# Shift-scale row on TensorE, sums moved between attention heads, a tenth pair of weight buffers

## The chip, the cores and the metric

The kernel runs on one core of a Trainium2 chip. Its time is the device time of one execution in microseconds (us), here 1450.13 us as the median of three executions (1447.05 to 1450.35). A core has TensorE (PE in the profile, matrix products, with PEld for its weight loads), VectorE (DVE, elementwise work and sums), ScalarE (ACT, activations and copies), GpSimd (POOL) and SyncE (SP). The engines run side by side and wait for each other by semaphores. Weights come from HBM by DMAs that SP and POOL issue; sixteen DMA engines carry them. Matrix results lie in eight banks of PSUM, everything else in SBUF.

## The reference

One layer of a diffusion transformer in float32, for 256 latent tokens and 256 context tokens of width 2048.

```
mod = silu(c) @ w_mod + b_mod                 # 6 parts of 2048: shift, scale, gate, shift, scale, gate
n_l = rmsnorm(x) * (1 + mod[1]) + mod[0]
z_l = n_l @ w_in                              # q, k, v, gMLP u and v, conv a and g
z_c = n_c @ w_in[:, k and v]                  # context tokens
out = concat(window_attention(q, k, v, k_c, v_c, sink),
             chunk_gmlp(u, v), conformer_conv(a, g)) @ w_out
h   = x + mod[2] * out
m   = rmsnorm(h) * (1 + mod[4]) + mod[3]
y   = grouped_moe(m)                          # router picks 2 of 16 experts per token
h   = h + mod[5] * y                          # expert e: silu(m @ w_gate) * (m @ w_up) @ w_down
```

Each expert has 24 MB of weights (w_gate, w_up and w_down, 8 MB each), and every expert that has tokens is read. The kernel moves 559.56 MB in all.

## The kernel before

**Order of the work.** `make_schedule` writes TensorE's order by hand. First come the modulation rows for shift and scale of the mixer, with the input projections for `a`, `g` and the first half of q (`Q0_`) between them. Then come the projections `KV_`, `Q1_`, `V_`, `U_` (16 steps of 128 rows each, four to a 1 MB chunk of weights), with the attention heads 0 to 7 spread over `Q1_` to `U_`, then `w_out` in 4 groups of 4 chunks (L753), the router (L772 to L821), the first expert job (always expert 15), and a loop over jobs. A job is one expert with a block of up to 96 of its tokens: 8 chunks of w_gate and 8 of w_up (L932 for up to 32 rows, L937 for 64), then 8 of w_down (L956, L962). The loop takes jobs in pairs, a small one that leads and a larger one.

**Buffers and who fills them.** SP issues all weights, in program order, so an issue that waits holds up those behind it. `ring` has 8 slots of 1 MB. Up to `w_out` the chunks of `CHUNK_STEPS` go round 6 of them; the other two (slots 6 and 7) hold four half-slots of 512 KB, which POOL fills with `w_half` for VectorE. For the expert jobs the memory is cut into pairs of 2 MB, `job_pairs`: 0 is ring slots 6 and 7, pairs 1, 2, 3 are slots 0 to 5, and pairs 4 to 8 lie over buffers that fall free in the course of the layer (`once` is pair 8). The first job uses nine of them (`first_pairs`), the loop six (`next_pairs`).

**The rest of the modulation.** The last four parts of the modulation go two ways. Part 5 (the gate of the experts) is made on TensorE, in 16 steps ("gate", L596) of four products each in four column groups. Parts 2, 3 and 4 are six halves of 1024 columns, and each half is a sum over 16 blocks of 128 rows: VectorE adds one block at a time, `sum_rows(n)` (L1311), 96 sums in all, and TensorE then sums over the partitions with a product with ones ("half", L583 for halves 0 and 1, L587 for 2 to 5). `sum_rows(n)` stands at fixed places in VectorE's program: 11 of the 96 ahead of head 1, 7 in the heads, 25 behind them, and 17, 16, 13 and 7 in the four groups of `w_out`.

**Who starts a half.** The two accumulators `halves` are used in turn. Before the first block of half i, POOL runs `start_half(i)` (L490, L492): it waits until half i-2 has been summed over the partitions by TensorE (`half_free`), clears the buffer and loads the bias, and only then issues that block (L498). POOL issues block m once VectorE has added block m-4. TensorE does half 0 right behind the scores of head 4 (`halves = {4: 0, 7: 1}`).

**Attention per head.** TensorE makes the scores (L687, L688), VectorE the maximum (`head_max`, L1445), ScalarE the exponentials, VectorE adds one block and then scales (`head_probs`, L1454), TensorE transposes the probabilities (L699) and multiplies by v (L706). Three steps of a projection (12 rows of the trace, L640) stand between scores and transposes.

## Time and profile before

| | |
|---|---|
| median of three executions | 1450.13 us (1447.05 to 1450.35) |
| the profiled execution | 1449.17 us, of which 1447.4 us are the span of the trace |
| PE busy | 1299.3 us (90%) |
| DVE busy | 423.1 us (29%) |
| ACT / POOL busy | 209.1 us / 73.6 us |
| DMA | 559.56 MB, mean 387 GB/s |
| mean granted TensorE clock | 0.975 of full speed |

How to read it: times in the trace count from the start of the span. The page cuts the span into 40 equal slices of 36.2 us; a digit is a busy share in tenths. A timeline row has start, duration, engine, line, operation, operands, count of merged instructions and, in brackets, how long the engine had been idle before it and what ended that. Ends of matmuls are modelled, so neighbouring rows overlap by up to 0.2 us; where it matters, starts are subtracted from starts. A row of the stretches has, for each engine, busy time and number of instructions, then the granted clock, the DMA share and GB/s. A row of the chain of waits in order of time has start, duration and what was on the chain.

### The profile page before, as it was taken

To read this page: it belongs to the slowest core of one execution; us is meant where nothing else is said; L and a number is where in the kernel's file an instruction comes from. 1 tells how busy PE (TensorE), PEld (TensorE's weight loads), DVE (VectorE), ACT (ScalarE), POOL (GpSimd) and SP (SyncE) were. 2 spreads that over 40 slices of the span, in tenths; PEclk is the share of its full clock that TensorE was granted. 3 is DMA by queue.
4 is the path that set the end of the run, shared out by engine and by line. 5 is a ranking of instruction groups with operands and counts; after the bars stand their busy time and mean duration, and the time that the engine had idled before them with its cause. 6 is when DMAs were issued, how large, how long until landed. Compare 5 with 4: busy or idle time off the path is not lost.

```text
span 1447.4 us, 20580 instructions
## 1 busy us (share of the span) xinstructions
PE 1299.3 (90%) x8742; PEld 618.0 (43%) x8743; DVE 423.1 (29%) x803; ACT 209.1 (14%) x488; POOL 73.6 (5%) x138
## 2 busy tenths in 40 slices
PE   6899999999989998999999999997887887878857
PEld 4556444545445465433632543442442442333223
DVE  2002885877666340202111201021110111111112
ACT  2002101343001133100200110110110110011001
POOL 0001301121322000000000000000000000000000
PEclk9999999999999899999999999999999999999988
DMA  9999659687998899999999999999999999999996
GB/s 380 409 420 384 252 233 397 217 279 271 346 377 313 334 368 426 427 426 424 427 427 415 418 428 427 411 428 427 429 427 428 427 430 428 429 429 428 427 428 263
DMA packets 57450, 559.56 MB, mean 387 GB/s; under 512 B 6688, under 2 KB 6816, under 8 KB 20768
## 3 DMA queue, kind: packets, MB, share of 16 engines
q1 hardware_dynamic: 42768, 504.35, 83.4%
q0 software_dynamic: 14320, 52.01, 9.9%
q10 hardware_dynamic: 288, 2.10, 0.3%
q8 instruction: 60, 0.98, 0.3%
q14 instruction: 14, 0.11, 0.0%
HBM read 556.34 MB, written 2.10 MB: 386 GB/s over the span
## 4 chain that ended last, share of the span: by engine, by line
PE 52%; DMA 39%; DVE 5%; issue 2%; ACT 1%; DVEq 0%; SPq 0%; ACTq 0%
DMA ring<-w_up_dram 11%; PE ps L932 9%; DMA ring<-w_gate_dram 9%; PE ps L937 8%; PE ps L640 7%; DMA ring<-w_half_dram 6%; PE ps L899 5%; PE ps L956 4%; DMA ring<-w_down_dram 4%; DMA big<-w_up_dram 4%; PE ps L962 3%; DVE once L1311 3%; DMA ring<-w_in_dram 3%; PE ps L634 2%; PE ps L645 2%
## 5 line engine op out<-in xcount | busy, mean ns | idle before, releaser
L1680 DVE TENSOR_TENSOR big<-ps,big 128x1024 f32<-128x1024 f32 x60 | 70.7, 1220 | 306.5 <-PE ps L885 161.0
L937 PE MATMUL ps<-ring,big 128*64 128x512 f32 x560 | 132.9, 608 | 22.1 <-DMA ring<-w_up_dram 10.6
L640 PE MATMUL ps<-ring,big 128*128 128x512 f32 x320 | 148.1, 602 | 2.9 <-DMA ring<-w_in_dram 2.3
L1311 DVE SCALAR_TENSOR_TENSOR once<-ring,silu_c,once 128x1024 f32<-128x1024 f32 x96 | 123.2, 1283 | 62.9 <-DMA ring<-w_half_dram 57.2
L899 PEld LDWEIGHTS ps<-probs,big 128*128 128x128 f32 x1024 | 119.2, 191 | 44.3 <-issue 37.6
L899 PE MATMUL ps<-probs,big 128*128 128x96 f32 x1024 | 129.8, 280 | 1.9 <-DVE probs L1684 1.9
L932 PE MATMUL ps<-ring,early 128*32 128x256 f32 x1408 | 90.4, 406 | 30.8 <-DMA ring<-w_up_dram 18.3
L753 PE MATMUL ps<-ring,big 128*128 128x512 f32 x240 | 109.5, 614 | 0.0
L640 PEld LDWEIGHTS ps<-ring,big 128*128 128x128 f32 x320 | 58.4, 191 | 70.4 <-issue 64.8
L937 PEld LDWEIGHTS ps<-ring,big 128*64 128x64 f32 x560 | 36.2, 137 | 104.6 <-issue 66.9
L962 PE MATMUL ps<-ring,once 128*64 128x512 f32 x336 | 77.5, 598 | 3.4 <-DMA ring<-w_down_dram 3.4
L932 PEld LDWEIGHTS ps<-ring,early 128*32 128x32 f32 x1408 | 44.3, 115 | 76.9 <-DMA ring<-w_up_dram 22.6
L956 PE MATMUL ps<-ring,once 128*32 128x512 f32 x576 | 73.2, 602 | 0.3 <-DMA ring<-w_down_dram 0.3
L753 PEld LDWEIGHTS ps<-ring,big 128*128 128x128 f32 x240 | 46.9, 198 | 56.9 <-issue 56.9
L1216 ACT ACTIVATE big<-ps,modcol,scale_ffn 128x96 f32<-128x96 f32 x112 | 39.1, 429 | 206.1 <-PE ps L899 206.1
L1712 DVE TENSOR_TENSOR once<-ps,early 128x512 f32<-128x512 f32 x12 | 8.3, 692 | 192.3 <-PE ps L956 125.4
L498 POOL DMA_DIRECT2D ring<-w_half_dram x96 | 51.1, 532 | 256.9 <-DVE once L1311 256.9
L1216 ACT ACTIVATE early<-ps,modcol,scale_ffn 128x96 f32<-128x96 f32 x144 | 50.3, 429 | 77.7 <-PE ps L899 77.7
L634 PE MATMUL ps<-big,ring 128*128 128x256 f32 x256 | 58.5, 382 | 1.6 <-DMA ring<-w_in_dram 1.6
L937 PE MATMUL ps<-big 128*64 128x512 f32 x224 | 52.4, 600 | 7.5 <-DMA big<-w_up_dram 5.0
L634 PEld LDWEIGHTS ps<-big,ring 128*128 128x128 f32 x256 | 47.8, 190 | 12.5 <-DMA ring<-w_in_dram 4.7
L932 PE MATMUL ps<-big,early 128*32 128x256 f32 x608 | 40.4, 414 | 13.9 <-DMA big<-w_up_dram 7.9
(320 smaller groups left out, 1094.0 us busy)
## 6 DMA issues: line engine op xcount, KB each, us to landing
ring<-w_down_dram SPq DMA_DIRECT2D x48, 2048.0 KB, 23.4
ring<-w_up_dram SPq DMA_DIRECT2D x46, 2048.0 KB, 23.0
ring<-w_gate_dram SPq DMA_DIRECT2D x33, 2048.0 KB, 22.1
ring<-w_half_dram POOLq DMA_DIRECT2D x96, 512.0 KB, 5.9
big<-w_up_dram SPq DMA_DIRECT2D x18, 2048.0 KB, 22.3
ring<-w_mix_dram SPq DMA_DIRECT2D x32, 1024.0 KB, 11.0
late<-w_down_dram SPq DMA_DIRECT2D x16, 2048.0 KB, 23.7
big<-w_gate_dram SPq DMA_DIRECT2D x15, 2048.0 KB, 25.4
```

The source lines that it names most:

```text
L498: pool.dma_start(half_slots[:, m % HALF_SLOTS, :], w_half[m]).then_inc(half_in[m % HALF_SLOTS], 16)
L634: mm = pe.matmul(Z[b + q // 2][:, (q % 2) * SEQ:(q % 2 + 1) * SEQ], w[:, q * P:(q + 1) * P], nT[:, k, 0:SEQ], start=(k == 0 and q % 2 == 0 ...
L640: mm = pe.matmul(ps[:, b + t, :], nT[:, k, t * P:(t + 1) * P], w, start=(k == 0), stop=(k == KT - 1))
L753: mm = pe.matmul(ps[:, b + t, :], mixT[:, k, t * P:(t + 1) * P], w[:, i, :], start=(k == 0), stop=(k == KT - 1))
L899: mm = pe.matmul(Yb[:, i, at:at + BLK], tokens[:, t, k * P:(k + 1) * P], one_hot[:, t, :], start=(t == 0), stop=(t == TT - 1))
L932: mm = pe.matmul(out_b[0][BASE * f:BASE * (f + 1), :], rows[0][:, k, :], w[:, kk, f * 256:(f + 1) * 256], start=(k == 0), stop=(k == KT - 1))
L937: mm = pe.matmul(out_b[1][REST * f:REST * (f + 1), :], rows[1][:, k, :], w[:, kk, f * N:(f + 1) * N], start=(k == 0), stop=(k == KT - 1))
L956: mm = pe.matmul(Db[0][BASE * q:BASE * (q + 1), :], hT[0][:, (i % 2) * P + BASE * (i // 2):(i % 2) * P + BASE * (i // 2 + 1)], w[:, q * N: ...
L962: mm = pe.matmul(Db[1][REST * (q // 2):REST * (q // 2 + 1), q % 2, :], hT[1][:, (i % 4) * P + REST * (i // 4):(i % 4) * P + REST * (i // 4 ...
L1216: last = act.activation(to[:, k, :], Yb[:, k // 4, at:at + BLK], ACT.Identity, bias=modcol[:, 3, k, 0:1], scale=scale_ffn[:, k:k + 1])
L1311: stt(total, half_slots[:, m % HALF_SLOTS, :], silu_c[:, m % KT, 0:1], total, ALU.mult, ALU.add) \
L1680: tt(y, Yb[:, 2 * h:2 * h + 2, :].rearrange("p a n -> p (a n)"), y, ALU.add).then_inc(summed, 1)
```

## The change

1. Half 5 (the second half of part 4, the scale of the experts' norm) leaves VectorE (`DVE_HALVES = 5`, 80 sums instead of 96). TensorE makes it in 8 steps ("scale"), two 128-row blocks to a 1 MB ring chunk, then turns it into columns ("scale_cols"); VectorE adds its bias. The 8 steps stand in `KV_`, where 8 of the 12 gate steps stood; those gates now stand in `Q1_`, three behind each of its four chunks. The sums over the conv channels ("convsum") move one chunk later.
2. The remaining 80 sums are spread otherwise: 21 ahead of head 1, 7 in the heads, 22 behind them, and 12, 9, 6 and 3 in the groups of `w_out`. POOL issues the first four blocks early. The last TensorE product of a half is half 4, behind `w_out` chunk (3, 1); before, it was half 5 there and half 4 behind (2, 2).
3. A tenth pair of buffers, `extra` (pair 9), takes the first 2 MB of the first job, issued before `Q1_`. From `V_` on the ring has 4 slots, so that pair 3 (slots 4 and 5) is issued in the middle of the projections. `first_pairs` and `next_pairs` are renumbered.
4. Room for `extra`: the scratch for POOL's DMA descriptors is set to 4096 bytes of a partition, `wr_scaled` lies in `late`, and four small tables are loaded into `silu_c` after the last sum.
5. In the first job the small product for the table of jobs (`table()`) stands after the fifth chunk of w_gate instead of after the eighth.

```
+DVE_HALVES = 5
@@ make_schedule
-    (KV_, 1): [("qT", 0)], (Q1_, 0): [("convsum",)], (Q1_, 1): [("kT",)], ...
+    (KV_, 1): [("qT", 0)], (Q1_, 0): [("scale_cols",)], (Q1_, 1): [("kT",), ("convsum",)], ...
             if g == KV_:
-                seq += [("gate", 3 * c + i) for i in range(3)]
-            elif g == Q1_ and c < 2:
-                seq += [("gate", 12 + 2 * c + i) for i in range(2)]
+                seq += [("gate", c), ("scale", 2 * c), ("scale", 2 * c + 1)]
+            elif g == Q1_:
+                seq += [("gate", 4 + 3 * c + i) for i in range(3)]
...
-             (2, 2): [("half", 4)], (3, 1): [("half", 5)], (3, 2): [("shift",), ("logits", 0), ...
+             (3, 1): [("half", 4)], (3, 2): [("shift",), ("logits", 0), ...
+NARROW, NARROW_SLOTS = NUMBER["win", V_, 0], 4
+PLACE = [(n - NPRE) % (PRE_SLOTS if n < NARROW else NARROW_SLOTS) for n in range(NPRE)]
@@ build
-        job_pairs += [nT_all[:, 0:2 * CH], big[:, TT * D:2 * TT * D], once[:]]
-        first_pairs = (0, 1, 8, 2, 3, 6, 7, 4, 5, 0, 1, 2)
-        next_pairs = (3, 4, 5, 0, 1, 2, 3, 4, 5, 0, 1, 2)
+        job_pairs += [nT_all[:, 0:2 * CH], big[:, TT * D:2 * TT * D], once[:], extra[:]]
+        first_pairs = (9, 0, 1, 8, 2, 3, 6, 7, 4, 5, 0, 1)
+        next_pairs = (2, 3, 4, 5, 0, 1, 2, 3, 4, 5, 0, 1)
@@ SP
+                if n == NARROW + NARROW_SLOTS:
+                    sp.wait_ge(slot_free, used_chunk(NARROW - 1))
+                    sp.dma_start(job_pairs[3], weights[5 // 4][FIRST_EXPERT, 5 % 4]) ...
+                if n == NUMBER["win", Q1_, 0]:
+                    sp.dma_start(job_pairs[first_pairs[0]], weights[0][FIRST_EXPERT, 0]) ...
-            for i in (5, 2, 0, 1, 3, 4, 6, 7, 8, 9, 10, 11):
+            for i in (6, 3, 1, 2, 4, 7, 8, 9, 10, 11):
...
                 elif s == 8:
-                    sp.wait_ge(half_free, 8)
+                    sp.wait_ge(half_free, 2 + DVE_HALVES)
                     sp.wait_ge(gatedT_done, 1)
-                    sp.wait_ge(half_step, HALF_SLOTS + 6 * KT)
+                    sp.wait_ge(half_step, HALF_SLOTS + DVE_HALVES * KT)
@@ TensorE
+                elif kind == "scale":
+                    for i in range(2):
+                        for h in range(2):
+                            at = 64 * h + 32 * i
+                            mm = pe.matmul(T[at:at + 32, :], silu_c[:, 2 * c + i, :],
+                                           slot(n)[:, (2 * i + h) * N:(2 * i + h + 1) * N], ...)
+                elif kind == "scale_cols":
+                    for q in range(4):
+                        mm = pe.matmul(T[:, 2 * q:2 * q + 2], modrow[:, 0, q * P:(q + 1) * P], k_("pick"), ...)
@@ VectorE, the places of sum_rows
-            sum_rows(2)
+            sum_rows(5)                               # ahead of the first norm of q
+            sum_rows(3)                               # behind the conv
+            sum_rows(2)                               # behind the norm of k
+            sum_rows(4)                               # ahead of convsum
-            sum_rows(5)
+            sum_rows(4)                               # behind convsum
-            sum_rows(3)
-            sum_rows(1)
+            sum_rows(3)                               # ahead of head 1
-                sum_rows((0, 2, 2, 5, 5, 5, 1, 5)[h])
+                sum_rows((0, 2, 2, 5, 5, 5, 1, 2)[h])
-                sum_rows((17, 16, 13, 7)[g])
+                sum_rows((12, 9, 6, 3)[g])
@@ kernel
-    nc = bacc.Bacc("TRN2", target_bir_lowering=False, num_devices=1)
+    nc = bacc.Bacc("TRN2", target_bir_lowering=False, num_devices=1, dynamic_dma_scratch_size=4096)
```

VectorE before, from the five sums behind head 3 to head 4; `SCALAR_TENSOR_TENSOR once<-ring` is one sum, `TENSOR_REDUCE small<-ps` the maximum of a head's scores:

```order
L1311 SCALAR_TENSOR_TENSOR once<-ring,silu_c,once 128x1024 [waits half_step,half_in2]
L1311 SCALAR_TENSOR_TENSOR once<-ring,silu_c,once 128x1024 [waits half_step,half_in3]
L1311 SCALAR_TENSOR_TENSOR once<-ring,silu_c,once 128x1024 [waits half_step,half_in0]
L1311 SCALAR_TENSOR_TENSOR once<-ring,silu_c,once 128x1024 [waits half_step,half_in1]
L1311 SCALAR_TENSOR_TENSOR once<-ring,silu_c,once 128x1024 [waits half_step,half_in2]
L1445 TENSOR_REDUCE small<-ps 128x2 [waits score_done,probs_done]
```

and the same place now:

```order
L1359 SCALAR_TENSOR_TENSOR once<-ring,silu_c,once 128x1024 [waits half_step,half_in0]
L1359 SCALAR_TENSOR_TENSOR once<-ring,silu_c,once 128x1024 [waits half_step,half_in1]
L1359 SCALAR_TENSOR_TENSOR once<-ring,silu_c,once 128x1024 [waits half_step,half_in2]
L1359 SCALAR_TENSOR_TENSOR once<-ring,silu_c,once 128x1024 [waits half_step,half_in3]
L1359 SCALAR_TENSOR_TENSOR once<-ring,silu_c,once 128x1024 [waits half_step,half_in0,bias_in]
L1496 TENSOR_REDUCE small<-ps 128x2 [waits score_done,probs_done]
```

The number of sums is the same, but the last of them is now block 32, the first of half 2 (it waits for `bias_in`); before it was block 28, and block 32 stood behind head 5.

SP before, from the chunks of `w_out` to the last of the first job:

```order
L438 DMA ring<-w_out_dram 128x2048 [waits slot_free] x16
L460 DMA big<-w_up_dram 128x4096 [waits slot_free]
L460 DMA once<-w_gate_dram 128x4096 [waits half_step,gatedT_done,half_free]
L460 DMA ring<-w_gate_dram 128x4096 [waits slot_free] x3
L460 DMA ring<-w_up_dram 128x4096 [waits slot_free]
L460 DMA big<-w_up_dram 128x4096 [waits slot_free]
L460 DMA big<-w_up_dram 128x4096 [waits logit_done]
L460 DMA late<-w_down_dram 128x4096 [waits cand_ready]
L460 DMA ring<-w_down_dram 128x4096 [waits slot_free] x3
```

and the same place now:

```order
L461 DMA ring<-w_out_dram 128x2048 [waits slot_free] x16
L483 DMA big<-w_up_dram 128x4096 [waits half_step,slot_free]
L483 DMA once<-w_gate_dram 128x4096 [waits half_step,gatedT_done,half_free]
L483 DMA ring<-w_gate_dram 128x4096 [waits slot_free] x2
L483 DMA ring<-w_up_dram 128x4096 [waits slot_free]
L483 DMA big<-w_up_dram 128x4096 [waits slot_free]
L483 DMA big<-w_down_dram 128x4096 [waits logit_done]
L483 DMA late<-w_down_dram 128x4096 [waits cand_ready]
L483 DMA ring<-w_down_dram 128x4096 [waits slot_free] x2
```

Ten issues stand behind `w_out` instead of twelve; two moved ahead of it (`extra`, and pair 3 in the ring).

## Rows read from the trace of the kernel before

**Rows 1.** The page: DMA rate in forty slices.

```profile
GB/s 380 409 420 384 252 233 397 217 279 271 346 377 313 334 368 426 427 426 424 427 427 415 418 428 427 411 428 427 429 427 428 427 430 428 429 429 428 427 428 263
```

**Rows 2.** Stretches, all engines: projections, slow clock, second pair of jobs.

```profile
260.00:280.00 20.00, 19.86 (x69) 10.67 (x68) 17.26 (x34) 8.77 (x21) 4.13 (x7) 1.00 0.64 221
...
480.00:485.00 5.00, 5.00 (x7) 1.99 (x7) 0.60 (x2) 0.00 (x0) 0.00 (x0) 0.53 0.86 308
...
780.00:800.00 20.00, 20.00 (x114) 4.49 (x112) 0.00 (x0) 0.00 (x0) 0.00 (x0) 1.00 0.98 398
```

**Rows 3.** The chain of waits in order of time, in the job loop.

```profile
711.48 1.92 PE ps L956 x16
...
831.70 1.92 PE ps L956 x16
...
972.34 22.66 DMA ring<-w_up_dram
```

**Rows 4.** Timeline of TensorE: a modulation row turned to columns; three gate steps.

```profile
109.99 0.95 PE L546 MATMUL ps<-const,modrow 128*128 128x2 f32 x8
...
199.71 2.78 PE L596 MATMUL ps<-ring,silu_c 128*32 128x512 f32 x24
```

**Rows 5.** Timeline of TensorE at heads 4 and 5.

```profile
298.76 1.05 PE L583 MATMUL ps<-once,const 128*32 128x512 f32 x4
...
305.70 1.09 PE L699 MATMUL ps<-const,probs 128*128 128x128 f32 x8 [0.54 <-DVE probs L1454]
...
319.75 1.09 PE L699 MATMUL ps<-const,probs 128*128 128x128 f32 x8 [2.20 <-DVE probs L1454]
```

**Rows 6.** Timeline of VectorE and of POOL (second row): head 0, starts of halves.

```profile
148.49 1.28 DVE L1311 SCALAR_TENSOR_TENSOR once<-ring,silu_c,once 128x1024 f32<-128x1024 f32 x1 [4.26 <-DMA ring<-w_half_dram]
...
142.99 0.95 POOL L490 MEMSET once<- 128x1024 f32 x1
...
250.51 1.23 DVE L1445 TENSOR_REDUCE small<-ps 128x2 f32<-128x1024 f32 x1 [1.30 <-PE ps L688]
...
254.28 0.88 DVE L1454 TENSOR_SCALAR probs<-probs,small 128x512 f32<-128x512 f32 x2
...
397.83 5.45 DVE L1311 SCALAR_TENSOR_TENSOR once<-ring,silu_c,once 128x1024 f32<-128x1024 f32 x4
408.63 4.06 DVE L1311 SCALAR_TENSOR_TENSOR once<-ring,silu_c,once 128x1024 f32<-128x1024 f32 x3 [5.36 <-DMA ring<-w_half_dram]
```

**Rows 7.** Timeline of TensorE in w_out.

```profile
377.04 13.90 PE L753 MATMUL ps<-ring,big 128*128 128x512 f32 x32
...
434.46 1.97 PE L766 MATMUL ps<-const,big 128*128 128x128 f32 x8 [4.75 <-DVE big L1529]
436.22 15.92 PE L753 MATMUL ps<-ring,big 128*128 128x512 f32 x32
451.98 1.84 PE L587 MATMUL ps<-const,once 128*128 128x1 f32 x16
...
476.96 2.81 PE L587 MATMUL ps<-const,once 128*128 128x1 f32 x16 [1.55 <-DVE once L1311]
...
489.17 0.93 PE L772 MATMUL ps<-late,modcol 128*1 128x16 f32 x31
```

**Rows 8.** Timeline of TensorE: the first job of the loop.

```profile
559.80 3.57 PE L932 MATMUL ps<-ring,early 128*32 128x256 f32 x32 [4.91 <-issue]
...
579.84 5.39 PE L932 MATMUL ps<-ring,early 128*32 128x256 f32 x96
```

**Rows 9.** Timeline of SP: its DMA issues (start, and time over which they were issued).

```profile
445.68 0.43 SPq L460 DMA_DIRECT2D big<-w_up_dram  x1
479.80 0.33 SPq L460 DMA_DIRECT2D once<-w_gate_dram  x1
...
535.97 0.35 SPq L469 DMA_DIRECT2D ring<-w_gate_dram  x1
```

**Rows 10.** The page, DMA issues: KB each, us to landing.

```profile
ring<-w_half_dram POOLq DMA_DIRECT2D x96, 512.0 KB, 5.9
```

104 lines of the change are left out of this document (70 added, 34 removed).

## The prediction

> **What bounds the kernel now.** I read the DMA rates first [rows 1]. From slice 15 on (520 us) they stay near 428 GB/s; between 140 and 340 us they are 217 to 397, and 221 in a typical stretch in which TensorE is busy 19.86 of 20 us [rows 2]. So up to the router TensorE and its waits set the time, and DMA has capacity left over. The loop must be read twice, since both are nearly full there. The chain of waits in order of time runs through TensorE from the first job of the loop to 970 us, and the same product recurs after 831.70 - 711.48 = 120.2 us [rows 3]. Two jobs are 24 pairs of 2.097 MB, 50.3 MB, 117.6 us at 428 GB/s. TensorE is 2.6 us the slower, and the rate shows it: it falls to 398 GB/s when the buffers are full [rows 2]. Behind 972 us the chain waits for DMAs, 22.66 us in the row [rows 3]. The DMAs there were held back by TensorE until about 920 us, so whatever time TensorE gains or loses before 920 us passes to the end once, and DMA time gained before the loop does not add to it.
>
> The terms are therefore TensorE's: its work, its idle time, and the slow stretch behind an idle time.
>
> **Work added.** Eight scale steps have the shape of gate steps (four products of 512 columns in four column groups). Three gate steps take 2.78 us [rows 4], so eight take 7.4 us. They keep the 3:1 pattern of `KV_`; the gates that they push out lengthen `Q1_`. The turn to columns is like the one for a modulation row, 0.95 us for four products [rows 4]. Together +8.3 us. The sum runs against the profiled execution, 1449.17 us; the median of the runs is 0.96 us above it.
>
> **A new stall at head 4.** Block 32 now stands on VectorE ahead of head 4's maximum. Its half can start only when TensorE has summed half 0, which follows the scores of head 4: at 298.76 us in the old trace, for 1.05 us [rows 5]. Behind that come POOL's clearing, bias and block 32. The trace has this piece elsewhere: from the clearing at 142.99 to the sum at 148.49 us, 5.5 us in light traffic [rows 6]. In heavy traffic it is longer: in `w_out` the fifth sum of a run, block 64, starts at 408.63, where the first, after which POOL starts that half, ended near 399.1 (a quarter of the 5.45 us from 397.83): 9.5 us [rows 6]. Around head 4 SP only has chunks to bring, and POOL's queue is empty, so I take 6.0. VectorE then needs 1.3 us for the sum and 4.65 us from maximum to probabilities (250.51 to 255.16) [rows 6]. From the start of half 0 that is 1.0 + 6.0 + 1.3 + 4.65 = 12.95 us. TensorE arrives at the transposes 305.16 - 298.76 = 6.4 us behind it [rows 5]. It waits 6.55 us, 6.0 more than the 0.54 now; by the bounds 5.5 to 9.5 more. Queued behind block 32 on VectorE are the maximum and the scaling of head 4, and TensorE, ScalarE's exponentials and all later heads wait for them.
>
> An idle TensorE comes back slowly. After 1.55 us of idleness its granted clock is 0.53 of full, close to the lower of its levels (1.2 of 2.4 GHz) [rows 2]; the 32 products behind the 4.75 us wait take 15.92 us instead of 13.90 [rows 7]. Behind the new stall I put 2.2 us, between 1.8 and 2.7 (both worked out below).
>
> The page gives a price for block 32 alone, 5.9 us to landing as the median of 96 [rows 10]. The Trainium skill ("DMA: Bandwidth & Descriptors", Anatomy of one DMA) has about 2.0 us fixed plus bytes at 436 GB/s for a DMA of POOL, an estimate of 3.2 us for 512 KB and would make the stall shorter. By it, with 1.8 us for clearing and bias, the piece would be 5.0 instead of 6.0 us and the sum below -5.45 instead of -4.45; the case's landing times are the longer ones, and the sum goes by them.
>
> **Waits that go.** `w_out` has 30 sums beside it instead of 53. VectorE itself waited for their DMAs, 5.36 us in the longest gap shown [rows 6]. At 434.46 TensorE had waited 4.75 us for VectorE, which had 13 to 17 sums to finish before each group's addition; now they are 12, 9, 6 and 3. A group of `w_out` is four chunks of 13.90/2 = 6.95 us [rows 7], 28 us, while nine sums with a late start take 9.5 + 8 x 1.3 = 20 us. This wait goes. With it goes its slow stretch: 451.98 - 434.46 = 17.52 us for what takes 13.90 + 0.9 at full clock, so 2.7. Sum -7.45 us. The second wait, 1.55 us for the last sum, goes too, and so does the product of the fifth half and its slow stretch: 489.17 - 476.96 = 12.21 us hold that product and 16 more, which alone are 6.95 [rows 7]. Sum -(1.55 + 5.3) = -6.8 us.
>
> **The job pairs.** Now SP stands at `once` until 479.80 us, when the last sum is done [rows 9]. Of the first job only one pair has been issued by then, at 445.68. Eleven follow, the DMA queue has a backlog, and the first pair of job 1, issued at 535.97 [rows 9], reaches TensorE at 559.80, after 4.91 us of idleness [rows 8]. With the change pair 9 and pair 3 come during the projections, where there is room, and `once`, pair 0 and pair 1 right behind half 4, some 15 us before the end of `w_out`. That is four pairs, 4 x 4.9 = 19.6 us of DMA, off the stretch behind 480 us. Job 1's pair then goes into a nearly empty queue and lands some 10 us before it is needed. The 4.91 us go, with the slow stretch: 32 instructions take 3.57 us where 96 take 5.39 (1.8 for 32) [rows 8], 1.8 us. Sum -6.7 us. Behind that TensorE's own pace is the limit, as shown.
>
> **At nothing.** Blocks 0 to 3 issued early add 2 MB around 131 us, when the ring is already ahead of TensorE; cover gone, it costs up to 4.9 us. Sums ahead of head 1 lie in VectorE's waits; the ten beyond the old eleven are 13 us of work against three idle times of 4 to 5 us and a `Q1_` that is 8 us longer. Four slots instead of six leave three chunks, 20.9 us, between issue and use of a chunk. `table()` moved is the same work, 2.6 us sooner, and DMA is not late there any more.
>
> The Trainium skill ("SBUF — State Buffer", SBUF size: 192, 224, or 256?) puts POOL's descriptor scratch at 16 KiB of a partition, and this change leaves 4. The Trainium skill ("DMA: Bandwidth & Descriptors", The descriptor swizzle) counts 9 descriptors per engine for a 128-partition transfer, so by it four blocks in flight need far less than 256 of 16 bytes, and nothing is charged.
>
> **Sum.** 8.3 + 6.0 + 2.2 - 7.45 - 6.8 - 6.7 = -4.45 us: 1444.7 on the profiled execution, 1445.7 us as a median. With the stall between its bounds 1445.2 to 1449.2; if the clock comes back faster or head 4's traffic is as light as at 143 us, down to 1443.
>
> **Rivals.**
> - *DMA rules the loop after all.* Then the lead of four pairs is kept to the end, less what DMA idles before the table of jobs is ready, about 15 us: 1435. For it speaks that the rates are within 3% of the highest [rows 1]. Against it: 120.2 against 117.6 us, and 398 GB/s at full buffers. 0.12.
> - *The stall eats the gain.* The restart takes 9.5 us or more, the clock 2.7, and head 5's wait of 2.20 us [rows 5] grows by a us or two because its blocks queue behind the late ones. 1449 to 1451, no measurable change. 0.22.
> - *Slower: VectorE falls behind for all later heads.* From head 4 each head's first block is requested late, and every head from 5 to 7 waits 3 us more on top of a stall of 9.5 + 2.7: 8.3 + 12.2 + 9 - 20.95 = +8.5, 1458.7. It decides if a block takes 9 us to land there, as one did in `w_out`, instead of 4 to 6. For it: the five sums behind each of these heads stay. Against it: by half 0 POOL has nothing else to bring, and three more blocks follow it at once. 0.1.
> - *The pairs don't come early enough.* `once` is held by half 4, and if the sums end as late as before, the wait at job 1 stays: -4.45 + 6.7 = +2.3, 1452.4. Against it: 23 fewer sums in that stretch. 0.06.
>
> My forecast has the other 0.5; half of it lies beyond 0.3% (4.35 us, about what a measurement of this kernel can tell from no change), since the sum is at that line. Faster: 0.27 + 0.12 and a little of the second = 0.42. Same: 0.23 + 0.2 = 0.43. Slower: 0.15. The forecast's own range is 1443 to 1449; the whole range is 1438 to 1453.
>
> **What would show it.** TensorE waits 5 to 10 us at the transposes of head 4 (for VectorE's probabilities), and VectorE as long for block 32 behind half 0. No wait for VectorE in `w_out`. The scores of the first head come about 5 us later than now, those of head 1 about 8. The router starts 2 to 4 us later than now. No idle time ahead of job 1. The job pairs recur after 120.2 us, with rates under 428 GB/s up to 920 us. I am wrong if the loop's period falls, if the wait at head 4 is missing, or if the waits in `w_out` stay.

## The result and the profile after

The kernel after takes 1465.63 us as the median of five executions (1462.43 to 1474.01), the kernel before 1450.29 beside it; the ratio is 1.0115, with a 95% interval of 1.0084 to 1.0147. It is slower by some 16 us, where 1445.7 was forecast. The profiled execution is the slowest of the five, 1474.01 us with a span of 1472.2, so the two traces differ by 24.8 us. In a second batch the same kernel had 1467.28 us against 1446.76 (1.0164, 1.0132 to 1.0197).

The page of after, DMA rate in forty slices of 36.8 us, answers to [rows 1]:

```profile
GB/s 380 400 421 416 233 313 417 418 208 231 301 324 223 312 350 398 428 427 382 370 426 403 361 424 428 378 429 428 427 428 428 430 429 428 428 428 428 429 427 267
```

In the job loop, where before had nothing under 411 until its last slice, there are 382, 370, 403, 361 and 378. DMA moved less there than before, and the loop's transfers wait for buffers that TensorE frees, so something held TensorE up in the loop. Ahead of the loop the predicted things are seen. TensorE of after, from `Q1_` over heads 2 and 4 to head 6 (answers to [rows 5]; L624 are gates, L744 the transposes of a head's probabilities, L686 a projection):

```profile
241.61 1.07 PE L624 MATMUL ps<-ring,silu_c 128*32 128x512 f32 x8 [1.68 <-DMA ring<-w_gmod_dram]
...
256.39 1.06 PE L624 MATMUL ps<-ring,silu_c 128*32 128x512 f32 x8 [2.02 <-DMA ring<-w_gmod_dram]
...
295.73 1.17 PE L744 MATMUL ps<-const,probs 128*128 128x128 f32 x8 [2.60 <-DVE probs L1505]
296.69 3.55 PE L686 MATMUL ps<-ring,big 128*128 128x512 f32 x4
...
329.42 1.97 PE L744 MATMUL ps<-const,probs 128*128 128x128 f32 x8 [6.46 <-DVE probs L1505]
331.18 3.37 PE L686 MATMUL ps<-ring,big 128*128 128x512 f32 x4
...
356.94 1.09 PE L744 MATMUL ps<-const,probs 128*128 128x128 f32 x8 [1.73 <-DVE probs L1505]
```

The stall at head 4 is 6.46 us long (6.55 was predicted). New are two waits for gate chunks and one at head 2 (295.73). VectorE and POOL of after around head 4 (POOL's row is the clearing for half 2; answers to [rows 6]):

```profile
317.69 0.95 POOL L513 MEMSET once<- 128x1024 f32 x1 [9.96 <-PE ps L611]
...
323.52 1.28 DVE L1359 SCALAR_TENSOR_TENSOR once<-ring,silu_c,once 128x1024 f32<-128x1024 f32 x1 [9.29 <-DMA ring<-w_half_dram]
324.72 1.22 DVE L1496 TENSOR_REDUCE small<-ps 128x2 f32<-128x1024 f32 x1
```

From clearing to sum are 5.83 us (6.0 was taken), and the maximum comes behind it. In `w_out` TensorE waits no more (answers to [rows 7]):

```profile
481.75 1.04 PE L811 MATMUL ps<-const,big 128*128 128x128 f32 x8
482.62 7.03 PE L798 MATMUL ps<-ring,big 128*128 128x512 f32 x16
489.49 1.84 PE L615 MATMUL ps<-const,once 128*128 128x1 f32 x16
```

The surprise stands in the jobs. TensorE of after at job 1 and at the head of the next two rounds of the loop (answers to [rows 8]; L975 are products of a small job, L944 gathers):

```profile
566.76 1.08 PE L975 MATMUL ps<-ring,early 128*32 128x256 f32 x8 [5.01 <-issue]
571.71 2.79 PE L975 MATMUL ps<-ring,early 128*32 128x256 f32 x24 [3.87 <-issue]
...
693.08 0.64 PE L975 MATMUL ps<-ring,early 128*32 128x256 f32 x8
697.27 2.79 PE L975 MATMUL ps<-ring,early 128*32 128x256 f32 x24 [3.55 <-issue]
699.99 3.73 PE L944 MATMUL ps<-probs,big 128*128 128x96 f32 x16
703.65 3.17 PE L975 MATMUL ps<-ring,early 128*32 128x256 f32 x32
...
824.44 1.63 PE L975 MATMUL ps<-ring,early 128*32 128x256 f32 x24 [3.19 <-issue]
```

Before runs through the same place without a stop (the 32 products of the second round, in one row):

```profile
681.02 1.93 PE L932 MATMUL ps<-ring,early 128*32 128x256 f32 x32
```

TensorE stops after eight products of a round, each time at the same instruction, and for nothing that the profile shows (`issue`). The trace records each float32 product of the kernel as two weight loads and two products, so the eight are 16 instructions. `issue` was the name in [rows 8] too. Behind the wait at 697 us the clock is at its lower level:

```profile
697.30:703.30 6.00, 6.00 (x39) 4.27 (x40) 0.00 (x0) 0.00 (x0) 0.00 (x0) 0.50 0.82 295
```

The two traces side by side, by the same instruction in each (us), with what the prediction's terms had made of it:

| | before | after | later by | predicted |
|---|---|---|---|---|
| start of `Q1_` | 219.06 | 220.20 | 1.1 | 0 |
| scores of head 1 | 259.79 | 274.02 | 14.2 | 8.3 |
| start of `w_out` | 359.78 | 383.64 | 23.9 | 16.5 |
| router | 498.42 | 507.49 | 9.1 | 2.3 |
| job 0, transposes | 538.11 | 544.55 | 6.4 | 2.3 |
| job 1, first down product | 591.21 | 603.31 | 12.1 | -4.45 |
| the same of job 3 | 711.48 | 730.84 | 19.4 | -4.45 |
| the same of job 5 | 831.70 | 856.99 | 25.3 | -4.45 |
| end of the span | 1447.4 | 1472.2 | 24.8 | -4.45 |

Of 24.8 us, 6.4 arise ahead of the jobs, 5.7 on the way to job 1, and 7.3 and 5.9 in the next two rounds of the loop (two jobs take 730.84 - 603.31 = 127.5 and then 126.2 us there, instead of 120.3 and 120.2). The 5.7 us belong with the rounds: before has one stop there, of 4.91 us, and after has a second one, of 3.87 us, eight products into the loop.

### The profile page after: what moved, and what is told of

It is laid out like the page before. It is cut to its first block, busy times and chain, and to the rows that moved or that the text cites. A ratio compares the mean times of both kernels' runs of the same rounds, so it can differ in the third digit from the quotient of the medians.

```text
span 1472.2 us, 20653 instructions
## 1 busy us (share of the span) xinstructions
PE 1306.7 (89%) x8798; PEld 620.7 (42%) x8799; DVE 401.9 (27%) x788; ACT 209.3 (14%) x488; POOL 65.3 (4%) x121
## 4 chain that ended last, share of the span: by engine, by line
PE 60%; DMA 33%; DVE 3%; issue 2%; ACT 1%; DVEq 0%; SPq 0%; POOL 0%; ACTq 0%
DMA ring<-w_up_dram 14%; DMA ring<-w_gate_dram 12%; PE ps L975 10%; PE ps L980 8%; PE ps L798 7%; PE ps L686 6%; PE ps L944 6%; PE ps L1001 5%; PE ps L1007 3%; DMA ring<-w_mix_dram 3%; PE ps L680 3%; DMA ring<-w_half_dram 2%; PE ps L691 2%; PE ps L930 1%; DMA ring<-w_gmod_dram 1%
## 5 line engine op out<-in xcount | busy, mean ns | idle before, releaser
L980 PE MATMUL ps<-ring,big 128*64 128x512 f32 x672 | 158.7, 606 | 26.0 <-DMA ring<-w_up_dram 15.6
L975 PE MATMUL ps<-ring,early 128*32 128x256 f32 x1664 | 111.5, 418 | 53.4 <-DMA ring<-w_up_dram 27.5
L686 PE MATMUL ps<-ring,big 128*128 128x512 f32 x320 | 151.0, 612 | 1.4 <-DMA ring<-w_in_dram 0.8
L944 PEld LDWEIGHTS ps<-probs,big 128*128 128x128 f32 x1024 | 123.4, 197 | 43.4 <-issue 36.7
L944 PE MATMUL ps<-probs,big 128*128 128x96 f32 x1024 | 134.0, 286 | 0.6 <-DVE probs L1738 0.6
L1359 DVE SCALAR_TENSOR_TENSOR once<-ring,silu_c,once 128x1024 f32<-128x1024 f32 x80 | 102.9, 1287 | 49.6 <-DMA ring<-w_half_dram 45.2
L975 PEld LDWEIGHTS ps<-ring,early 128*32 128x32 f32 x1664 | 53.6, 118 | 111.5 <-issue 37.0
L980 PEld LDWEIGHTS ps<-ring,big 128*64 128x64 f32 x672 | 43.5, 137 | 124.1 <-issue 80.0
L686 PEld LDWEIGHTS ps<-ring,big 128*128 128x128 f32 x320 | 59.5, 195 | 70.7 <-issue 66.0
L1007 PE MATMUL ps<-ring,once 128*64 128x512 f32 x224 | 51.9, 598 | 2.3 <-DMA ring<-w_down_dram 2.3
L521 POOL DMA_DIRECT2D ring<-w_half_dram x80 | 42.6, 533 | 216.4 <-DVE once L1359 216.0
L1282 ACT COPY once<-ps 128x256 f32<-128x256 f32 (+1 forms) x19 | 8.3, 451 | 305.0 <-PE ps L995 305.0
L1460 DVE SCALAR_TENSOR_TENSOR once<-yT,late,once 128x256 f32<-128x256 f32 x120 | 47.6, 475 | 0.0
L1001 PE MATMUL ps<-ring,once 128*32 128x512 f32 x384 | 47.4, 600 | 0.0
```

The lines of the kernel that those rows point to most:

```text
L686: mm = pe.matmul(ps[:, b + t, :], nT[:, k, t * P:(t + 1) * P], w, start=(k == 0), stop=(k == KT - 1))
L944: mm = pe.matmul(Yb[:, i, at:at + BLK], tokens[:, t, k * P:(k + 1) * P], one_hot[:, t, :], start=(t == 0), stop=(t == TT - 1))
L975: mm = pe.matmul(out_b[0][BASE * f:BASE * (f + 1), :], rows[0][:, k, :], w[:, kk, f * 256:(f + 1) * 256], start=(k == 0), stop=(k == KT - 1))
L980: mm = pe.matmul(out_b[1][REST * f:REST * (f + 1), :], rows[1][:, k, :], w[:, kk, f * N:(f + 1) * N], start=(k == 0), stop=(k == KT - 1))
L1001: mm = pe.matmul(Db[0][BASE * q:BASE * (q + 1), :], hT[0][:, (i % 2) * P + BASE * (i // 2):(i % 2) * P + BASE * (i // 2 + 1)], w[:, q * N: ...
L1007: mm = pe.matmul(Db[1][REST * (q // 2):REST * (q // 2 + 1), q % 2, :], hT[1][:, (i % 4) * P + REST * (i // 4):(i % 4) * P + REST * (i // 4 ...
```

## Experiments

**What is being told apart.** Between the products on both sides of a stop there is a transfer of 16 KB on the queue that the profile calls instruction. The DMA view of after from 694.8 to 696.0 us (queue and kind: packets, MB, share):

```profile
q1 hardware_dynamic: 20, 0.29, 63.6%
q8 instruction: 1, 0.02, 4.9%
```

Its packet starts at 694.92, 1.6 us behind TensorE's last instruction (693.34), and ends at 695.87; TensorE goes on at 697.27. The page counts 63 of them in after and 60 in before, of 16,384 bytes each; in straight code one comes every 250 instructions or so (products and weight loads). Theory A: a boundary between two loaded pieces of code lies 16 instructions behind the loop's head, and the jump back finds the first piece loaded and the second not. The Trainium skill ("Runtime: NRT & Kernel Launch", Instruction fetch mechanics) says that code comes in blocks of 256 instructions and that a taken branch breaks the sequential prefetch; the packets' size and spacing agree. Rival B: the loop is held up by its transfers, since pairs were renumbered and DMA's rate fell. A shift of the code that changes no work tells them apart.

**after_shift40.** Nothing but waits that are already met, at a place where TensorE is idle:

```
             pe.wait_ge(const_in, 16)
+            for _ in range(80):
+                pe.wait_ge(const_in, 16)
             pe.wait_ge(silu_done, 1)
```

The 80 waits are 40 instructions (the page counts 20,693 instead of 20,653).

> The kernel after, with 40 more instructions in TensorE's program, all of them waits that are already met, issued at its start where TensorE is idle for 12 us. No work is changed; every later instruction lies 40 places further on in the program. Theory A (code loading): in the trace of after the first product of a loop round stops 16 instructions behind the loop's first one, at 693.7, 821.3 and 567.8 us, and goes on 1.4 us after a 16 KB transfer of the instruction queue has ended; a boundary between two loaded pieces of code lies there, and the shift moves it some 230 instructions behind the loop's head. The waits of 3.87, 3.55 and 3.19 us and the slow stretches behind them go, two jobs take 120.2 us again instead of 127.5, and the time falls by 12 to 18 us, to 1447 to 1453. The wait of 5.0 us at the jump into the loop stays. Rival B (the other order of the buffer pairs, or the transfers, hold the loop up): the waits stay and the time is 1462 to 1469.

1456.47 us against 1447.43, ratio 1.0069 (1.0045 to 1.0093), where after had 1.0115; 3.5 us more than the range that theory A had. The stops at the loop's head are gone; the one ahead of job 1 stays. TensorE at job 1 and at the next round:

```profile
565.24 3.51 PE L977 MATMUL ps<-ring,early 128*32 128x256 f32 x32 [4.86 <-issue]
...
686.42 1.93 PE L977 MATMUL ps<-ring,early 128*32 128x256 f32 x32
688.98 2.02 PE L946 MATMUL ps<-probs,big 128*128 128x96 f32 x16 [0.62 <-DVE probs L1740]
```

The same down products recur after 716.88 - 596.65 = 120.2 us. Buffers, transfers and work are those of after, and the stops are gone, so theory A holds. Against the two batches of after, 1.0115 and 1.0164, 40 instructions that do nothing make the kernel 7 to 14 us faster. Another 9 us over before remain (1456.47 against 1447.43): they arise ahead of the jobs, since the stretch behind job 0's transposes is no longer than in before (907.9 and 909.3 us).

**before_shift49.** The same lines in the kernel before, with `range(98)`.

> The kernel before, with 49 more instructions in TensorE's program (waits already met, in its first idle time), so that its loop's head stands against the boundaries of the loaded code as in the kernel after. Theory A: it gets what after has: a second wait of 3 to 4 us, 16 instructions into the loop, at each round of it until DMA rules (three or four of them, some 6 to 7 us each with the slow clock behind), so 1462 to 1470 us. Rival B (pairs or transfers): no change, 1447 to 1452.

1448.14 us, 1.0007 (0.9985 to 1.0030): no change, so my expectation failed. The cause was my count. The stop in this trace is 0.27 us and stands 79 instructions behind the loop's head, not 16. A float32 product is two weight loads and two products in TensorE's program; the change had moved the head by 112 places, not by 49.

The trace has one more stop, which no other trace has in this size: TensorE enters the second of its job loops (from job 7 on) at 917.82 us and stops behind 22 products, with a 16 KB packet of the instruction queue inside the wait (919.01 to 919.98 us):

```profile
917.82 1.50 PE L934 MATMUL ps<-ring,early 128*32 128x256 f32 x22
921.34 1.40 PE L934 MATMUL ps<-ring,early 128*32 128x256 f32 x10 [2.03 <-issue]
```

It fits with theory A that a shift lays a boundary there too. It was not tried apart.

**before_shift112.** The same with `range(224)`.

> The kernel before, with 112 more instructions in TensorE's program (waits already met, issued in its first idle time). A product of float32 turned out to be four instructions there (two weight loads, two products), so the change's eight scale steps had moved the loop's head by 112 places and not 49; with 49 the boundary lay 79 instructions behind the head and cost 0.27 us. With 112 it should lie 16 behind it, as in the kernel after. Theory A (code loading): a wait of 3 to 4 us, 16 instructions into each round of the loop, two jobs take 126 to 128 us instead of 120.2, and the time is 10 to 18 us over before. Rival B: no change, since nothing else of the kernel after is in it.

1459.33 us, 1.0088 (1.0062 to 1.0113). The kernel before, with nothing of the change in it, now has the waits of after. The 224 waits outlast the idle time at the start (TensorE's first product begins at 15.81 us instead of 12.02), but job 0 starts at 538.0 us as in before, so that is not what costs. TensorE at job 1 and the next two rounds (L934 are products of a small job):

```profile
559.69 1.08 PE L934 MATMUL ps<-ring,early 128*32 128x256 f32 x8 [4.90 <-issue]
564.12 2.79 PE L934 MATMUL ps<-ring,early 128*32 128x256 f32 x24 [3.35 <-issue]
...
684.76 0.64 PE L934 MATMUL ps<-ring,early 128*32 128x256 f32 x8
688.40 1.50 PE L934 MATMUL ps<-ring,early 128*32 128x256 f32 x24 [3.00 <-issue]
...
810.76 1.50 PE L934 MATMUL ps<-ring,early 128*32 128x256 f32 x24 [2.62 <-issue]
```

Two jobs take 717.74 - 594.99 = 122.75 us here, not 127.5. The stop is 3.0 us and the 24 products behind it take 1.50 us, the full clock, where after took 2.79. With that the effect of the code's place is shown from both sides, and rival B is out.

**after_again.** The kernel after, unchanged.

> The kernel after once more, unchanged, beside the next one. In its profiled run the three waits at the loop's head were followed by products at half clock, so that two jobs took 127.5 us; in before_shift112 the same waits had no slow stretch behind them at 688 us and two jobs took 122.4. Theory A (the wait is there each time, the slow clock behind it in some executions): the waits of 3 to 4 us are at the same places, the period is between 122.4 and 127.5, and the median is 1459 to 1466, since after_shift40, without the boundary, was 1456.5. Rival (something else of the kernel after makes its loop slower than that of before_shift112): the period is 127 to 128 again.

1467.28 us, profiled 1463.34. The waits are in the same places, 3.98, 2.96 and 2.75 us, and two jobs take 723.00 - 600.29 = 122.7 us. TensorE at the next round, and its stretch behind the stop:

```profile
693.66 1.50 PE L975 MATMUL ps<-ring,early 128*32 128x256 f32 x24 [2.96 <-issue]
```

```profile
693.70:699.70 6.00, 6.00 (x79) 4.22 (x80) 0.00 (x0) 1.40 (x4) 0.00 (x0) 1.00 0.98 393
```

The stop is there in both traces, the clock's fall behind it at these two rounds only in the first: behind job 0 the first takes 927.6 us and this one 918.4, which is the larger part of the difference between the first trace's 24.8 us and the medians' 15. The waits ahead of the jobs differ too: head 4 waits 6.34 us and gate chunks 1.09 and 2.32 again, but head 2 waits for nothing over 1 us. The median was 1.3 us over my range.

```
                 with pe.If(few):
+                    if first:
+                        block_of_few, spot = nc.cur_bb, pe.mark_branch_hint_location()
                     experts(j, (0,), first)
+                if first:
+                    bass.BassInstruction(block_of_few.bb.instructions[-1]).branch_hint(spot)
```

```profile
557.62 1.91 PE L932 MATMUL ps<-ring,early 128*32 128x256 f32 x32
...
585.17 3.20 PE L932 MATMUL ps<-big,early 128*32 128x256 f32 x32 [2.96 <-DMA big<-w_up_dram]
```

**pairs_only.** The change without its scale steps:

```
-DVE_HALVES = 5
+DVE_HALVES = 6
-                seq += [("gate", c), ("scale", 2 * c), ("scale", 2 * c + 1)]
-            elif g == Q1_:
-                seq += [("gate", 4 + 3 * c + i) for i in range(3)]
+                seq += [("gate", 3 * c + i) for i in range(3)]
+            elif g == Q1_ and c < 2:
+                seq += [("gate", 12 + 2 * c + i) for i in range(2)]
...
-                sum_rows((12, 9, 6, 3)[g])
+                sum_rows((17, 16, 13, 7)[g])
```

> The change without its scale steps: the tenth pair of buffers, the ring of four from V on, the earlier job pairs, the first four blocks ahead and table() moved stay; all 96 sums are on VectorE again and in the old places (5 instead of 2 stand first). The loop's head lies as in the kernel before. Theory A (from 540 us on the time is set by TensorE with six pairs of buffers, so pairs brought earlier change nothing): 1446 to 1452 us, no change against before. Rival (the prediction's step: the early pairs end the wait ahead of job 1): 1440 to 1444. Second rival (the narrow ring or the earlier pairs cost TensorE waits in Q1 and V): 1453 to 1458.

1450.42 us, 1.0021 (1.0001 to 1.0040). From job 0's transposes to the end it takes 1448.3 - 538.35 = 909.9 us, before 1447.4 - 538.11 = 909.3. The tenth pair, the narrow ring and the earlier issues bring nothing and cost at most a few us.

**pairs_hint.** Both together.

> pairs_only with the branch hint of before_hint. In before_hint the wait of 4.9 us ahead of job 1 was gone, but job 1 then waited 2.96 and 0.32 us for pairs of weights, and the time fell by 1 us only. Theory A (two limits lie behind each other there: the loading of code, and behind it the pairs): with both lifted the stretch from job 0's last transposes (L993) to job 1's first down product (L1002), 53.8 us in pairs_only, is 49 us, as in after_v2 with both, and the time is 3 to 6 us under pairs_only and under before. Rival (the pairs come when their buffers are free, whatever is issued early): 52 us in that stretch and 1 us under before, as in before_hint.

1448.74 us, 1.0012 (0.9997 to 1.0027). The stretch to job 1's down product is 582.32 - 533.95 = 48.4 us, as theory A had it, 5 us less than in pairs_only. But the time did not follow, so its conclusion is wrong: the next pair of jobs takes 706.55 - 582.32 = 124.2 us instead of 120.2. TensorE, 5 us ahead, waits there for DMA, as these rows show:

```profile
596.39 1.92 PE L1002 MATMUL ps<-ring,once 128*32 128x512 f32 x16 [0.34 <-DMA ring<-w_down_dram]
601.14 1.61 PE L976 MATMUL ps<-ring,big 128*32 128x256 f32 x16 [2.82 <-DMA ring<-w_gate_dram]
```

**after_s40_extra.** after_shift40 with the tenth pair issued in `U_`:

```
-                if n == NUMBER["win", Q1_, 0]:
+                if n == NUMBER["win", U_, 4]:
```

> after_shift40, and the tenth pair of the first job (2 MB) is issued in the group U instead of ahead of Q1. Theory A: TensorE's waits for gate chunks in Q1 (1.68 and 2.02 us, and about 1 us of slow clock) come from that pair, which costs 4.9 us of DMA just where three gates go with every chunk; they go, and the time is 3 to 5 us under after_shift40. Rival: three gates and a chunk to every 10 us are themselves too much for the ring and the waits stay: no change.

1455.33 us, 1.0062 (1.0038 to 1.0086), against 1.0069: no difference. The waits for gate chunks are 1.86 and 2.01 us. The rival was right; the 2 MB ahead of `Q1_` are not their cause.

**after_s40_sums.** after_shift40 with other numbers of sums behind heads 3 to 7:

```
-                sum_rows((0, 2, 2, 5, 5, 5, 1, 2)[h])
+                sum_rows((0, 2, 2, 3, 5, 6, 1, 3)[h])
```

> after_shift40, and the sums behind heads 3 to 7 are 3, 5, 6, 1, 3 instead of 5, 5, 5, 1, 2: block 32, which waits for half 0, stands behind head 4's probabilities instead of ahead of its maximum. Theory A (the stall at head 4 is that block): TensorE's wait of 6.46 us at the transposes of head 4 and its slow stretch of 2.4 us go; head 5 or 6 may wait 1 to 3 us, since a sixth sum stands there. 5 to 8 us under after_shift40. Rival (VectorE is late for these heads whatever the order): the wait moves to head 5 in full, and the time stays within 2 us.

1454.97 us, 1.0056 (1.0037 to 1.0075): 1.5 to 2 us under after_shift40, where 5 to 8 were expected. The stall at head 4 is gone, and half of it is back at head 5:

```profile
324.26 1.04 PE L746 MATMUL ps<-const,probs 128*128 128x128 f32 x8
...
339.11 1.93 PE L746 MATMUL ps<-const,probs 128*128 128x128 f32 x8 [3.05 <-DVE probs L1507]
```

In this execution the gate chunks cost more (0.93, 0.78 and 2.03 us, with waits for projection chunks of 0.5 us behind). The stall was block 32, as predicted, but putting it off by two sums does not pay.

**after_v2.** after_s40_sums with the hint, and gates in `V_`. (VectorE's addition of the gate's bias, which waits for the last gate, moves from behind head 1 to behind head 2 with them; not shown.)

```
-                seq += [("gate", 4 + 3 * c + i) for i in range(3)]
+                seq += [("gate", 4 + 2 * c + i) for i in range(2)]
+            elif g == V_ and c < 2:
+                seq += [("gate", 12 + 2 * c + i) for i in range(2)]
```

> after_s40_sums with two more edits: the branch hint of before_hint, and the last gates spread (two with each chunk of Q1 and two with the first two chunks of V instead of three with each of Q1). Theory A: the wait of 4.6 us ahead of job 1 and its slow stretch go (6 us), and the waits for gate chunks in Q1 (0.9 to 2.0 us each, some 5 us with the slow clock) shrink to under 2 us in sum, so 8 to 10 us under after_s40_sums: 1445 to 1447. Rival: the gates only shift the lack of DMA into V, where blocks and chunks wait instead, and only the hint counts: 1448 to 1450.

1458.43 us, 1.0074 (1.0046 to 1.0102): neither theory. The waits moved and grew: 3.62 us at head 0, 2.71 at a gate in `V_`, 2.12 and 4.83 at later heads. In `V_` the ring has four slots and the heads wait as well; it looks like no place for more chunks, though with three edits at once the run doesn't show which of them costs.

**after_v3.** The gates go the other way, into `KV_`, where DMA moved only 252 and 233 GB/s before (slices 5 and 6 of [rows 1]); the halves' products stand one head earlier; fewer sums stand in the heads. The shift by 40 and the hint are in it too:

```
-                seq += [("gate", c), ("scale", 2 * c), ("scale", 2 * c + 1)]
+                seq += [("gate", 2 * c), ("gate", 2 * c + 1), ("scale", 2 * c), ("scale", 2 * c + 1)]
             elif g == Q1_:
-                seq += [("gate", 4 + 3 * c + i) for i in range(3)]
+                seq += [("gate", 8 + 2 * c + i) for i in range(2)]
-    halves = {4: 0, 7: 1}
+    halves = {3: 0, 6: 1}
-                sum_rows((0, 2, 2, 5, 5, 5, 1, 2)[h])
+                sum_rows((0, 2, 2, 4, 4, 4, 1, 2)[h])
-                sum_rows((12, 9, 6, 3)[g])
+                sum_rows((13, 10, 7, 3)[g])
```

> The kernel after, shifted by 40 instructions and with the hint, and with its order of work mended: two gates and two scale steps with each chunk of KV, two gates with each of Q1 (instead of one and three); the products of halves 0 and 1 behind heads 3 and 6 instead of 4 and 7; four sums behind heads 3 to 5 instead of five, and 13, 10, 7, 3 in w_out instead of 12, 9, 6, 3. Theory A (the change's own terms are sound, and what it lost are four things: the code boundary, the sum that waits for half 0, three gates to a chunk of Q1, and heads with too many sums): no wait over 1.5 us at heads 3 to 6, under 1 us at gates, job 0's first transposes at 525 to 530 us instead of 544.5, and 1434 to 1442 us in all. Rival (VectorE and DMA have no room for the sums and chunks in this stretch, so the waits only change their place, as in after_s40_sums and after_v2): 1448 to 1453.

1439.04 us (1436.54 to 1442.25) against 1446.59, ratio 0.9950 (0.9935 to 0.9965): faster than both kernels. Heads 2 to 7 have no wait, and no gate is waited for; 2.33 us stay at head 0 and 0.93 at head 1. TensorE at half 0 and head 4, and at job 0's transposes:

```profile
301.11 1.05 PE L613 MATMUL ps<-once,const 128*32 128x512 f32 x4
...
319.85 1.04 PE L746 MATMUL ps<-const,probs 128*128 128x128 f32 x8
...
530.68 0.44 PE L994 MATMUL ps<-const,once 128*128 128x128 f32 x2 [0.61 <-DVE once L1758]
```

**after_v4.** The same without the edits to halves and sums.

> The kernel after, shifted by 40 instructions, with the hint and with the gates moved (two with each chunk of KV, two with each of Q1) but with the halves and sums as in after. Theory A (the stall at head 4 comes from the half and not from the gates): the wait of 6.5 us at head 4 stays, the waits at gates in Q1 go, and the time is 9 to 12 us over after_v3. Rival: the longer KV gives VectorE so much time that the head's waits shrink too, within 4 us of after_v3.

1450.98 us, 1.0035 (1.0022 to 1.0049), 12 us over after_v3: theory A. Head 4 waits 6.19 us. The gates' waits are gone in both, so of the mended order the half's place and the number of sums bring the larger part. (The two were not tried apart.)

**v3_unshifted.** The order of after_v3, without shift and hint.

> after_v3 without the shift and without the hint: its order of work alone, with the loop's head at the place of the kernel after. Theory A (the boundary costs the same whatever stands ahead of the loop): it has the waits of 4.9 and 3 to 4 us at job 1 and of 3 to 4 us at each round, and is 6 to 13 us over after_v3, 1446 to 1452. Rival (after_v3 gains by its order alone, because an earlier router leaves DMA a lead): 1439 to 1443.

1452.09 us, 1.0044 (1.0024 to 1.0065), 13 us over after_v3, at the upper end of what was expected. TensorE stops 4.80 and 3.56 us at job 1, and 3.36 and 2.80 us at the next two rounds:

```profile
682.55 2.79 PE L975 MATMUL ps<-ring,early 128*32 128x256 f32 x24 [3.36 <-issue]
685.27 3.73 PE L944 MATMUL ps<-probs,big 128*128 128x96 f32 x16
```

The better order gains 7 us on before, if the loop lies well; the bad place of the loop costs 13, the missing hint included (alone it was worth 1 to 2 us in the kernels before and pairs_only).

**All traces in one table.** Job 0 is the start of its transposes, the rest is the span behind it, two jobs is the distance of the down products of jobs 1 and 3 (us).

| | job 0 | rest | two jobs | boundary behind the head |
|---|---|---|---|---|
| before | 538.1 | 909.3 | 120.3 | 128 |
| before_hint | 541.0 | 909.1 | 120.8 | 127 |
| pairs_only | 538.4 | 909.9 | 120.2 | 128 |
| pairs_hint | 534.0 | 908.8 | 124.2 | 127 |
| after_shift40 | 543.2 | 907.9 | 120.2 | 232 |
| after_s40_extra | 542.4 | 909.7 | 120.2 | 232 |
| after_s40_sums | 541.7 | 908.8 | 120.2 | 232 |
| after_v2 | 549.6 | 908.4 | 123.7 | 231 |
| after_v3 | 530.7 | 907.9 | 123.5 | 231 |
| after_v4 | 540.1 | 908.0 | 123.4 | 231 |
| before_shift49 | 533.5 | 912.1 | 120.6 | 79 |
| before_shift112 | 538.0 | 918.5 | 122.8 | 16 |
| after_again | 543.1 | 918.4 | 122.7 | 16 |
| v3_unshifted | 530.3 | 922.8 | 127.6 | 16 |
| after | 544.6 | 927.6 | 127.5 | 16 |

(The boundary is counted in the built program; at 16 and 79 it is where the traces show the stop.) The rest is 908 to 910 us wherever the boundary is far from the head, with or without early pairs, tenth pair or hint. With the boundary at 79 it is 912.1, of which the stop at the second loop is the larger part, and at 16 it is 918.4 to 927.6. So the time is two numbers: when job 0 gets there, and what the code's place adds. The first is known to a few us only from one trace: before, before_hint and the two shifted kernels before have the same work ahead of job 0 and start it between 533.5 and 541.0 us; after and its runs with the same order (after_again, after_shift40, after_s40_extra) between 542.4 and 544.6.

Only the first loop pays. In a round of it TensorE has 1024 recorded products and as many weight loads, and instruction packets come all through it (28 of them from 577 to 946 us in after). In a round of the second loop there are 703 of each, and between 1010 and 1370 us the queue has not one packet, in any of the 15 traces. Products and weight loads by stretch in after:

```profile
566.76:693.08 126.32, 119.99 (x1024) 49.32 (x1024) 14.44 (x23) 13.66 (x38) 0.00 (x0) 0.96 0.99 408
1089.52:1208.65 119.13, 96.62 (x703) 42.82 (x703) 16.90 (x31) 13.11 (x36) 0.00 (x0) 0.96 1.01 429
```

So a loop of some 1400 of these instructions ran without loading code again, and one of some 2050 did not. A shorter loop body would be another way out; it was not tried.

## Why the prediction was wrong

**Work added: right.** From the start of `Q1_` to head 1's scores TensorE takes 13.1 us more; 8.35 were put for the added steps, 3.7 are the two waits for gate chunks (see below), 1 us is left.

**The new stall at head 4: right.** 6.46 us of waiting, 5.92 more than before, for 6.0; the products behind it take 2.3 us longer, for 2.2. Block 32 caused it, as after_s40_sums and after_v3 show, in which it is gone.

**Waits that go in `w_out`: right.** From its start to the router 123.85 us instead of 138.64, 14.8 less, for 14.25.

**"At nothing": wrong in part.** Three gates with each chunk of `Q1_` cost 3.7 us of waiting; I had counted their products and not their 3 MB to a chunk's 1 MB. Head 2 waits 2.60 us, with 1.7 us of slow products. (In after_shift40 it is 1.95 us, in after_again under 1.) The sum ahead of its maximum waited for a block that POOL had issued 14 us ahead (issue at 275.41, sum at 289.42 after 2.86 us of idleness), where the page's median landing is 5.9. Against that, head 5's wait of 2.20 us and its slow stretch went, probably since the stall ahead had let VectorE catch up (not tried), and the router's stretch ran at full clock. In sum +6.4 us at job 0 in these two traces instead of +2.3, and some 9 us by the medians of after_shift40. The places of the halves and the number of sums in the heads were the costliest part of this, and could have been better: after_v3 is 12 us faster than after_v4.

**The job pairs: this step failed.** I put the 4.91 us ahead of job 1 down to a late pair of weights, and -6.7 us to its going. The row names "issue": TensorE waited for nothing that the profile shows. The landing of that very pair, in the trace of before, which I had not looked up, says it was no DMA (the issue at 535.97 us):

```profile
ring<-w_gate_dram SPq DMA_DIRECT2D x1, 2048.0 KB, 11.7
```

It was there at 547.7, 12 us before TensorE went on. before_hint took the wait away by a hint alone. pairs_only and pairs_hint show besides that early pairs are worth nothing, with that wait or without: the rest behind job 0 stays 909 to 910 us. So the term is worth nothing: in after_shift40 job 1's down product comes 596.65 - 543.19 = 53.5 us behind job 0's transposes, in before 591.21 - 538.11 = 53.1. The +5.7 us of after on this way are the stop of 3.87 us that the code's place brought.

**"Behind that TensorE's own pace is the limit": this step failed too.** The pace was taken to be given. The loop's period went from 120.3 to 127.5 us, by instructions that stand far ahead of the loop. No term of mine was for the place of code; I had the 60 transfers of the instruction queue on the page and did not ask what they meant at a jump. Of the loss this is the larger part in the first trace, where the stretch behind job 0 takes 927.6 us against 907.9 in after_shift40, and about half of it by medians: 7 to 14 us (after_shift40 against after, after_v3 against v3_unshifted), where some 9 arise ahead of the jobs.

**Rivals.** DMA rules the loop: half true and without effect on this change. By the prediction's own numbers it has only 2.6 us to spare in two jobs, which may be why most of the 5 us of the hint come back in a pair of jobs of 124.2 us. The stall eats the gain: no, its price was right. VectorE late for all later heads: it was late at heads 2, 4 and 6, by 2.60, 6.46 and 1.73 us, not for all. The pairs don't come early enough: they came early, and it did not matter. The direction of the slower rival was right, its mechanism was not.

## What to carry to other kernels

A wait that the profile gives to "issue", in a program with branches, is a question about code before it is one about data: look for a transfer on the instruction queue inside the wait, and look up when the data had landed. A change ahead of a long loop moves the loop in the program; before blaming the change, shift the old kernel by the same number of instructions (a float32 product counts four) and the new one away from it, with waits already met in idle time. And prefetching more than the loop's buffers hold gives nothing if the loop is bound by TensorE: what counts is when the first job starts. If a loop's stops are code, its length matters as well: the shorter of two loops here loaded nothing while it ran.

## What the runs showed of the hardware

- A stop of 2.6 to 4.0 us at each round of the first loop (1024 products and 1024 weight loads recorded in a round), if a boundary between 16 KB pieces of TensorE's code lies 16 instructions behind the loop's head (twelve stops in four traces); 0.27 us at 79, none seen at 127 and more.
- The jump over the two variants of job 0 cost 4.5 to 5.0 us without a hint, 0 to 2.0 with one.
- A loop with 703 products and 703 weight loads in a round loaded no code from 1010 to 1370 us, in all traces; the first loop loaded code in each round.
- The clock behind such a stop: at full in before_shift112, after_again and v3_unshifted (2.62 to 3.00 us of idleness), at 0.50 in after (3.55 us), with products as slow (2.79 us for 24) behind 3.35 to 3.98 us elsewhere. In after a wait of 2.60 us at head 2 was followed by slow products as well, so the length of the wait alone does not tell.
- From the 28th to the 37th of the forty slices DMA moves 427 to 430 GB/s in all kernels. Those whose boundary is far from the loop's head take 908 to 910 us for what is left behind job 0's transposes, whatever is changed ahead.
